# Key numbers of the gate one-hots in PSUM, and one broadcast comparison for four tokens

## What is computed

```python
s = einsum('nhjd,hjkd->nhjk', q, sub_keys)          # 8 heads, 2 halves, 128 keys each
sv, si = top_k(s, 16)                                # per half
cand = sv[:, :, 0, :, None] + sv[:, :, 1, None, :]   # 16 x 16 sums
tv, ti = top_k(cand, 16)
eidx = take(si0 * 128 + si1, ti)                     # 8 x 16 experts out of 16384 per token
gate = softmax(tv)
a = einsum('tkd,td->tk', u_tab[eidx], h)
out = einsum('tk,tkd->td', gate * gelu(a), v_tab[eidx])
```

## Time and profile before

| | |
|---|---|
| runs | 3432.83, 3429.09, 3430.80 us; median 3430.8 |
| profiled execution | span 3435.4 us from the first to the last instruction; no time around it is given |
| mean granted TensorE clock | 0.923 |
| busy | TensorE 3014.2 us (88%), weight loads 2849.4 (83%), VectorE 2246.2 (65%), ScalarE 1199.6 (35%), GpSimd 1489.5 (43%) |
| one-hots | L1057 2304 x 509 ns mean, L1055 768 x 292 ns mean |
| gate stages | 644 to 1216 us and 2276 to 2848 us |

### The profile page before, as it was taken

How to read it: one execution, slowest core, us unless ns; L and a number is a source line. 1 busy time by engine, 2 the same in 40 slices (tenths; PEclk the granted TensorE clock), 3 DMA queues, 4 the chain that set the end, 5 groups by cost and what they waited for, 6 DMA issues and landing times.

```text
span 3435.4 us, 56066 instructions
## 1 busy us (share of the span) xinstructions
PE 3014.2 (88%) x18256; PEld 2849.4 (83%) x18256; DVE 2246.2 (65%) x5088; ACT 1199.6 (35%) x1619; POOL 1489.5 (43%) x641
## 2 busy tenths in 40 slices
PE   4677699789898999999997769978989899999998
PEld 1365599688888899999986559968888889999998
DVE  0146679999999933333334667999999993444444
ACT  0132335343333333333333233533333333333332
POOL 0042347333343455555544134733434344555554
PEclk8787899899999999999998789989999999999999
DMA  8913205345544477777750320534554447666665
GB/s 334 391 56 136 111 26 161 100 130 174 166 160 167 154 254 245 236 238 245 242 158 2 137 110 26 162 101 126 177 166 160 167 154 249 220 219 223 220 219 168
DMA packets 287521, 591.79 MB, mean 172 GB/s; under 512 B 25908, under 2 KB 210356, under 8 KB 277464
## 3 DMA queue, kind: packets, MB, share of 16 engines
q1 hardware_dynamic: 108064, 386.85, 34.4%
q10 hardware_dynamic: 179384, 204.02, 17.7%
HBM read 483.30 MB, written 107.50 MB: 172 GB/s over the span
## 4 chain that ended last, share of the span: by engine, by line
PE 36%; DVE 34%; issue 15%; DMA 11%; ACTq 2%; ACT 1%; DVEq 1%; POOL 0%; SPq 0%; PEldq 0%
DVE oh L1057 13%; DMA gin<-gate_scratch 9%; PE ps L1417 6%; PE ps L1418 6%; PE ps L1422 6%; DVE oh L1055 4%; DVE wv L1076 3%; PE ps L1316 2%; PE ps L1311 2%; PE ps L1312 2%; DMA wada<-in_wada 2%; PE ps L1368 1%; PE ps L1369 1%; DVE ti L1011 1%; DVE rs L864 1%
## 5 line engine op out<-in xcount | busy, mean ns | idle before, releaser
L1057 DVE TENSOR_SCALAR oh<-cst,iT,gP 128x128 bf16<-128x128 f32 x2304 | 1047.2, 509 | 0.0
L416 POOL TENSOR_TENSOR uring_lo<-uring,uhi 128x1024 fp32r<-128x1024 f32 x256 | 635.9, 2485 | 842.4 <-ACT uhi L427 842.4
L420 POOL TENSOR_TENSOR vring_lo<-vring,vhi 128x1024 fp32r<-128x1024 f32 x256 | 610.7, 2396 | 466.1 <-ACT vhi L427 463.8
L1368 PE MATMUL ps<-hh,uhi 128*128 128x384 f32 x2048 | 739.2, 361 | 3.2 <-ACT uhi L427 3.2
L1369 PE MATMUL ps<-hl,uhi 128*128 128x384 f32 x2048 | 714.0, 349 | 0.0
L1417 PE MATMUL ps<-wvhi,vhi 128*128 128x384 f32 x2048 | 685.6, 335 | 5.8 <-DVE wv_lo L1078 3.8
L1418 PE MATMUL ps<-wv_lo,vhi 128*128 128x384 f32 x2048 | 685.1, 335 | 0.0
L1076 DVE TENSOR_TENSOR wv<-ain,gin 128x768 f32<-128x768 f32 x128 | 286.1, 2235 | 592.8 <-DMA gin<-gate_scratch 413.8
L427 ACT ACTIVATE uhi<-uring 128x1024 fp32r<-128x1024 f32 x256 | 271.5, 1061 | 521.4 <-PE ps L1369 507.8
L1368 PEld LDWEIGHTS ps<-hh,uhi 128*128 128x128 f32 x2048 | 412.7, 202 | 3.6 <-issue 3.6
L1369 PEld LDWEIGHTS ps<-hl,uhi 128*128 128x128 f32 x2048 | 410.0, 200 | 0.0
(11 more groups left out here) (215 smaller groups left out, 3123.4 us busy)
## 6 DMA issues: line engine op xcount, KB each, us to landing
uring<-in_uT SPq DMA_DIRECT2D x256, 512.0 KB, 4.1
vring<-in_vt SPq DMA_DIRECT2D x256, 512.0 KB, 4.2
wada<-in_wada SPq DMA_DIRECT2D x12, 4096.0 KB, 14.8
act_scratch<-aout ACTq DMA_DIRECT2D x128, 384.0 KB, 4.6
gate_scratch<-gst ACTq DMA_DIRECT2D x48, 1024.0 KB, 6.1
ain<-act_scratch ACTq DMA_DIRECT2D x128, 384.0 KB, 3.5
gin<-gate_scratch ACTq DMA_DIRECT2D x128, 384.0 KB, 5.0
wpq<-in_wpq SPq DMA_DIRECT2D x4, 4096.0 KB, 12.2
```

What stands on the lines that cost most here:

```text
L416: sub(uring[s][1][:], uring[s][0][:], uhi[s % 2][:].bitcast(F32), ALU.subtract).then_inc(u_lo, 1)
L420: sub(vring[s][1][:], vring[s][0][:], vhi[s % 2][:].bitcast(F32), ALU.subtract).then_inc(v_lo, 1)
L1057: ins = ts(oh[s][:, k, n, :], iota, iT[:, tok], gP[n][:, tok], ALU.is_equal, ALU.mult)
L1368: mm(out, uhi[s % 2][:, k, :], hh[:, k, :], start=(k == 0), stop=False)
```

## The change

After `iota` is known in a layer, it is copied into PSUM bank 7 (`iota_ps`), and all comparisons read it there. The four unscaled one-hots of a round are no longer one comparison with a scalar each, but one comparison of tensors: the key numbers, repeated four times, with the four columns of `jT`, each repeated 128 times. The scaled ones stay three a token, with the same scalars.

```diff
         ps = ctx.enter_context(nc.psum_tensor("ps", [P, 8, 512], F32))
+        iota_ps = ps[:, 7, 0:NKEY]
@@
                 iota = cst[:, C_IOTA:C_IOTA + NKEY]
                 step(nc.vector.tensor_copy(iob[:], iota[:, 0:TOPK]), chain)
+                step(nc.vector.tensor_copy(iota_ps, iota), chain)
@@
                     if not first:
                         dve.wait_ge(g_pe, 2 * i + (s - 1 + gb))
+                    quad = bass.ds(2 * TOK * i + TOK * s, TOK)
+                    keys = iota_ps.unsqueeze(1).broadcast_to([P, TOK, NKEY])
+                    tt(oh[s][:, :, GP, :], keys, jT[:, quad].unsqueeze(2).broadcast_to([P, TOK, NKEY]), ALU.is_equal)
                     for k in range(TOK):
                         tok = bass.ds(2 * TOK * i + (TOK * s + k), 1)
-                        ins = ts(oh[s][:, k, GP, :], iota, jT[:, tok], None, ALU.is_equal)
                         for n in range(GP):
-                            ins = ts(oh[s][:, k, n, :], iota, iT[:, tok], gP[n][:, tok], ALU.is_equal, ALU.mult)
+                            ins = ts(oh[s][:, k, n, :], iota_ps, iT[:, tok], gP[n][:, tok], ALU.is_equal, ALU.mult)
                     ins.then_inc(oh_done, 1)
```

## The result

The kernel takes 3222.7 us (median of 4 runs, 3216.55 to 3225.78) against 3431.82 before (4 runs). The ratio is 0.9383, 95% interval 0.9366 to 0.9400. The profiled execution took 3223.51 us, with a span of 3221.7 and a mean granted clock of 0.944.

What follows compares the result with a forecast made beforehand. VectorE was taken to bound the gate stage at 6.00 us a step; without its stall TensorE's 4.92 would bound. Saving 104.4 us a layer, 208.8 in all, gives span 3226.6 and forecast 3222 us, own range 3212 to 3235.

Steps and rivals of the forecast that it cites:

- The bound and its cause: Gate stage: VectorE bounds at 6.00 us a round, 3.87 of work and 2.13 of stall during GpSimd's subtraction.
- Why PSUM frees it: Gate-stage compares: only instructions reading twice from SBUF at a time wait; reading PSUM removes the 2.13 us stall a round.
- The costs: VectorE's gate round: twelve scaled compares 3.96 us plus one broadcast comparison 0.62, sum 4.58, bounds 3.74 and 5.56.
- The spare time: Gate stage: VectorE's 4.58 us a round ends 0.34 before TensorE's 4.92.
- A fixed cost for PSUM: VectorE's thirteen PSUM instructions a round: by the skill's rule 0.84 us more, round 5.43, kernel near 3319.
- The sum: Both layers: 104.4 us saved in each, 208.8 together; span 3435.4 to 3226.6, forecast median 3222.
- the start: Start of each layer's gate stage: gates begin at 642.9 instead of 644.31, 1.4 us saved.
- the clock behind the last wait: Behind each layer's last gates: no slow TensorE clock any more, 1.4 us saved.
- A: Rival, VectorE's gate compares: PSUM reads do not overlap or cost more in succession; up to 3344 us; chance 0.14.
- B: Rival, gate stage: the stall behind GpSimd stays, 6.71 us a round, kernel 3566; chance 0.04.
- C: Rival, gate stage: TensorE without waits does not keep clock or pace, 5.41 us a step, kernel 3315; chance 0.05.

## Why the prediction held

**The bound and its cause.** Confirmed. VectorE's 6.00 us a round were 3.87 of work and 2.13 of waiting for GpSimd: with half the subtraction half of the waiting went, and the step fell to 4.90 without any change to a comparison.

**Why PSUM frees it.** I argued from instructions in the output projection that what waits is a second reading of SBUF. The run with 123 key numbers shows for the comparisons that the place of the operand is not what counts: from SBUF at one element a time, none was held. The run with a broadcast comparison out of SBUF shows the other kind, two SBUF inputs, being held. The Trainium skill, "SBUF — State Buffer", in the section on who interferes with whom, has just these two kinds as those that contend with GpSimd, and an instruction with one SBUF input outside the modes that take two ports (which handle two elements at a time or more) as free; the traces of these two runs (0.46 us held, and 411 ns at most) agree.

**The costs.** A scaled comparison was put at 0.405 long and 0.33 apart, and measured 0.402 and 0.319. The broadcast one was put at 0.62 and measured 0.60. The round came to 4.43 against 4.58. TensorE's step came to 4.90 against 4.92. The spare time, put at 0.34, is 0.47.

**A fixed cost for PSUM.** The Trainium skill, "VectorE: DVE Perf Modes", in the section on the TRN2 errata, gives a PSUM source 62 cycles more than an SBUF source, by which I had estimated 5.43 a round. The trace does not agree: the same comparison is 394 ns for 123 elements out of SBUF and 402 for 128 out of PSUM, 8 ns apart, of which, as an estimate with the 0.96 GHz of that table, the five elements are 5. Nor does it follow less closely: twelve start 0.309 apart out of SBUF ((3.79 - 0.39) / 11) and 0.319 out of PSUM.

**The sum.** Per layer 103.3 us were saved between first and last gate matmul (101.6 forecast), 0.8 at the start (1.4 forecast). At the second layer's first gates the kernel is 106.8 ahead (2275.99 against 2169.15), 2.7 more than at the first layer's last (1214.72 against 1110.59, 104.1), against 1.4 forecast for the clock behind the last wait. The span fell by 213.7 against 208.8. Most of the difference is the 0.02 in the step, 190 x 0.02 = 3.8.

That the median of 3222.7 lies within 1 us of the 3222 is in part luck, of two errors that cancel. The span came out 4.9 below the forecast (3221.7 against 3226.6). But the 4.6 that I took off to get from the profiled span to the median of the runs held how slow that one execution happened to be, and is no fixed amount: after the change the median lies 1.0 above the profiled span.

**The rivals.** A (comparisons from PSUM follow each other less closely) needed 0.36 apart; they are 0.319 apart. B (the stall stays) needed 1.42 of 2.13; nothing stays. It does stay, with its 2.1 us, when the scaled comparisons go back to SBUF with two elements at a time. C (the clock): 1.00 in the stage.

One thing the prediction did not say: half of the change is idle. The broadcast comparison gives 0.43 us a round to VectorE (4.86 against 4.43), where VectorE no longer bounds. By the prediction's own costs it would have been needed: 12 x 0.33 and 4 x 0.27 make 5.04, 0.12 over TensorE's 4.92. It was not, since a comparison came to 0.319 and left 0.04 to spare.

## What to carry to other kernels

An engine that is full in the profile may be waiting inside its instructions: compare the shortest and the longest of one form, and look what the engine next to it does in the long ones. Here slower instructions (402 instead of 339 ns) made the stage 18% shorter, because GpSimd no longer held them; forcing one element at a time in SBUF did the same as moving the operand to PSUM. Once another engine bounds, count the spare time of the freed one before trimming it further: here it is 0.47 us of 4.90, and the second half of the change paid nothing.

## What was not expected of the hardware

- A hold can lock to the pace of the bounding engine. The broadcast comparison with two SBUF inputs was held in nearly every round by 0.46 us, the spare time, and cost nothing.
- The clock does not fall after every wait of the same length. After the change it fell behind those of 2.73 and 2.65 us (the step behind the first takes 6.49 instead of 4.90, at a granted clock of 0.74), but behind waits of 2.29 to 2.35 us in the run with only the broadcast comparison in PSUM it fell 14 times of 52. With short waits in nearly every step, 5.07 a step instead of 4.90, it stayed at 1.00.
- Small instructions of the ranking pay for the stall in proportion most: a copy of 8 elements takes 913 ns on the mean, and 359 with half the subtraction. After the change, in layer 0, its three runs take 171, 172 and 2365 ns, so the mean is one held instruction among two free ones.
